# A two-layer hybrid block and a mixture of experts: units of the first gate moved into gated linear attention, three sparse items left without a weight unit

## The reference

```python
def hybrid_mixer(h, ...):
    (hq, hf, hi, hog, gq, gk, gv, glr, gog,
     nq_, nkc, nvc, nks, nvs, nkw, nvw, ngate, mgate) = split_cols(h @ w_in)
    ...
    y_hg = head_rmsnorm(o_hg, hg_norm_g, h.dtype) * jax.nn.silu(hog)
    log_a = jax.nn.log_sigmoid((glr @ gla_w2 + gla_b).astype(jnp.float32)) / GLA_TAU
    o_gla = chunked_gated_linear_attention(heads(gq, GLA_HEADS) * GLA_DK ** -0.5, heads(gk, GLA_HEADS),
                                           heads(gv, GLA_HEADS), heads(log_a, GLA_HEADS))
    y_gla = head_rmsnorm(o_gla, gla_norm_g, h.dtype) * jax.nn.silu(gog)
    ...
    y_nsa = nsa_attention(q, kc, vc, ks, vs, kw, vw, gates)
    g = jax.nn.sigmoid(mgate).reshape(B, T, N_BRANCH, D_MODEL)
    m = (g[:, :, 0] * (y_hg @ w_br_hg) + g[:, :, 1] * (y_gla @ w_br_gla)
         + g[:, :, 2] * (y_nsa @ w_br_nsa))
    return m @ w_out
```

## Time and profile before

| quantity | value |
|---|---|
| median of 3 runs | 2077.39 us (2074.11 to 2078.36) |
| the profiled execution's own time | 2070.91 us |
| its span, first to last instruction | 2069.1 us |
| TensorE busy, share of the span | 1986.2 us, 96% |
| VectorE busy | 1446.2 us, 70% |
| ScalarE busy | 1035.8 us, 50% |
| mean granted TensorE clock | 0.986 |
| second linear attention to the start of the rotation, layer 0 | about 136 to 196 us |
| sparse items, layer 0 | about 245 to 328 us |

### The profile page before, as it was taken

The page is one execution under the profiler, slowest core; times in us unless marked ns, Lnnn a source line. Parts: engine busy times, 40 slices in busy tenths (PEclk is TensorE's granted clock), DMA queues, the critical chain, the costliest instruction groups (busy, mean ns, idle before and its releaser), DMA issues.

```text
span 2069.1 us, 40471 instructions
## 1 busy us (share of the span) xinstructions
PE 1986.2 (96%) x17190; PEld 1942.8 (94%) x17190; DVE 1446.2 (70%) x2389; ACT 1035.8 (50%) x1480; POOL 8.7 (0%) x17
## 2 busy tenths in 40 slices
PE   7899999999989999999999899999899999999998
PEld 7899999999989899999999889999889999999998
DVE  5867777787578777768756757777759775665554
ACT  5754554544375555545444454444366664444443
POOL 0000000000000000000000000000000000000000
PEclk9999999999999999999999999999999999999999
DMA  6433533697544343348865236788725423365552
GB/s 208 132 114 103 194 113 132 216 321 260 182 143 133 124 158 118 124 173 285 305 203 191 92 109 227 292 310 295 287 90 174 154 94 111 122 202 187 192 193 93
DMA packets 101844, 370.18 MB, mean 179 GB/s; under 512 B 11552, under 2 KB 11936, under 8 KB 101536
## 3 DMA queue, kind: packets, MB, share of 16 engines
q1 hardware_dynamic: 100368, 363.38, 51.7%
q10 hardware_dynamic: 1296, 4.21, 0.6%
HBM read 366.50 MB, written 1.05 MB: 178 GB/s over the span
## 4 chain that ended last, share of the span: by engine, by line
PE 57%; DVE 22%; DMA 9%; ACT 7%; issue 5%; SPq 0%; ACTq 0%; DVEq 0%
PE ps L378 15%; PE ps L380 15%; PE ps L379 15%; DVE low L315 7%; DMA ada_rows<-in_ada 5%; DMA raw<-in_stream 4%; ACT high L312 3%; DVE ada_rows L2107 3%; PE ps L609 1%; DVE sq L3058 1%; PE ps L658 1%; PE ps L2039 1%; PE ps L1599 1%; PE ps L3143 1%; PE ps L912 1%
## 5 line engine op out<-in xcount | busy, mean ns | idle before, releaser
L315 DVE TENSOR_TENSOR low<-raw,high 128x1024 fp32r<-128x1024 f32 x590 | 717.6, 1221 | 368.5 <-ACT high L312 367.5
L378 PE MATMUL ps<-hh,high 128*128 128x256 f32 x2832 | 803.6, 284 | 23.2 <-DVE low L315 16.0
L312 ACT CAST high<-raw 128x1024 fp32r<-128x1024 f32 x590 | 612.7, 1047 | 423.9 <-PE ps L380 324.1
L379 PE MATMUL ps<-hh,low 128*128 128x256 f32 x2832 | 788.4, 278 | 0.0
L380 PE MATMUL ps<-hl,high 128*128 128x256 f32 x2832 | 788.2, 278 | 0.0
L378 PEld LDWEIGHTS ps<-hh,high 128*128 128x128 f32 x2832 | 535.5, 189 | 32.7 <-issue 17.6
L379 PEld LDWEIGHTS ps<-hh,low 128*128 128x128 f32 x2832 | 535.6, 189 | 1.2 <-issue 0.5
L380 PEld LDWEIGHTS ps<-hl,high 128*128 128x128 f32 x2832 | 535.7, 189 | 0.0
L378 PE MATMUL ps<-ffn_high,high 128*128 128x256 f32 x672 | 192.1, 286 | 4.2 <-DVE ffn_low L2126 4.2
L379 PE MATMUL ps<-ffn_high,low 128*128 128x256 f32 x672 | 189.3, 282 | 0.0
L380 PE MATMUL ps<-ffn_low,high 128*128 128x256 f32 x672 | 189.2, 281 | 0.0
(11 more groups left out here) (468 smaller groups left out, 2816.6 us busy)
## 6 DMA issues: line engine op xcount, KB each, us to landing
raw<-in_stream SPq DMA_DIRECT2D x590, 512.0 KB, 4.2
ada_rows<-in_ada SPq DMA_DIRECT2D x96, 512.0 KB, 5.4
c_act<-in_c SPq DMA_DIRECT2D x3, 512.0 KB, 4.3
bias<-in_bias ACTq DMA_DIRECT2D x1, 1536.0 KB, 8.7
xT<-in_xT SPq DMA_DIRECT2D x4, 256.0 KB, 5.6
out<-xT SPq DMA_DIRECT2D x4, 256.0 KB, 2.1
par<-in_par ACTq DMA_DIRECT2D x1, 842.0 KB, 11.2
hybrid_const<-in_const ACTq DMA_DIRECT2D x1, 800.0 KB, 5.9
```

The lines of the kernel that those rows point to most:

```text
L312: return act.copy(self.high[:, slot, :], self.raw[:, slot, :])
L315: return dve.tensor_tensor(self.low[:, slot, :], self.raw[:, slot, :], self.high[:, slot, :].bitcast(F32), ALU.subtract)
L378: pe.matmul(out, sh, mh, start=start, stop=False, **more)
L379: pe.matmul(out, sl, mh, start=False, stop=False, **more)
```

## The change

In the second linear attention the plan is filled differently: step 0 has three units instead of two, steps 1 to 6 have one each, step 7 none, and step 8 the second half of the last pair; the pair that stood between the sums of squares and the spreading is gone from there. All constant products of this call go (6, 9 and 3 a layer). The first two units of `Mix`, the two halves of the first gate, move into the end of this stage: TensorE does one before the values and one after them, and ScalarE and VectorE treat both at the very end of their programs for this stage. The gate's result goes to a bank of `banks` instead of `mix_banks`. `rope` keeps three units (the next three), `compress` has eight instead of seven, `compressed_probabilities` three, and the sparse items 16 instead of 19: items 4, 7 and 10 have none. The ring gets 11 units of mix before the compression's weights instead of 8. The first linear attention, which calls the same function, stays as it was.

```diff
+            gates_ahead = mix.take(2) if mix is not None else ()
...
                     for p in tail[1:]:
                         proj.vector(dve, p)
+                    for p in gates_ahead:
+                        mix.vector(dve, p)
...
                     for p in tail[1:]:
                         proj.scalar(act, p)
+                    for p in gates_ahead:
+                        mix.scalar(act, p)
...
                         for p, only in plan[step]:
                             proj.tensor(pe, mine[p], only)
+                    for p in gates_ahead[:1]:
+                        mix.tensor(pe, p)
...
                     tell(ins, pv_done)
-                    keep_busy(pe, 6, 3)
+                    for p in gates_ahead[1:]:
+                        mix.tensor(pe, p)
+                    if mix is None:
+                        keep_busy(pe, 6, 3)
...
-                        self.gate[n] = Product(w, i * BLOCKS, 2, KD, mix_banks)
+                        self.gate[n] = Product(w, i * BLOCKS, 2, KD, mix_banks if n else banks)
...
-                return self.mine[0:2] if i < 0 else self.mine[i + 2:i + 3]
+                return [p for p, at in zip(self.mine, (-1, -1, 0, 1, 2, 3, 5, 6, 8, 9, 11, 12, 13, 14, 15, 16)) if at == i]
...
-            mine, last = taken[:5], taken[5:]
+            mine, last = taken[:6], taken[6:]
...
+            mix = Mix()
+            mix.claim(11)
             linear_attention(gq, gk, gv, gg, GLA_H * GLA_DK // P, GLA_DK, gog, P1("gla_norm", layer), 1, proj,
-                             [[(0, None)], [(1, 0)], [(1, 1)], [(2, 0)], [(2, 1)], [], [], [], [(3, None)]], 1,
-                             {1: 6, LEVELS: 9})
+                             [[(0, None), (1, 0)], [(1, 1)], [(2, 0)], [(2, 1)], [(3, 0)], [(3, 1)], [(4, 0)], [], [(4, 1)]], 0,
+                             {}, mix)
...
-            mix = Mix()
-            mix.claim(8)
             windows = ring.claim(4)
-            mix.claim(len(MIX_ORDER) - 8)
+            mix.claim(len(MIX_ORDER) - 11)
             rope(mix, 3)
-            compress(windows, mix, 5 + 2)
+            compress(windows, mix, 6 + 2)
             compressed_probabilities(mix, 3)
-            sparse_attention(mix, 19)
+            sparse_attention(mix, 16)
```

10 lines of the change are left out of this document (6 added, 4 removed).

## The result

| | kernel before | changed kernel |
|---|---|---|
| median of 4 runs each, taken together | 2075.87 us | 2097.66 us (2092.77 to 2105.49) |
| ratio | | 1.0104, 95% interval 1.0085 to 1.0123 |
| the profiled execution's own time | 2070.91 us | 2092.77 us |
| its span | 2069.1 us | 2091.0 us |
| mean granted TensorE clock | 0.986 | 0.979 |

The change makes the kernel 1.0% slower. The span grew by 21.9 us where the sum had 14.1.

The account below looks back on a forecast made before the run. TensorE, busy 1986.2 of 2069.1 us, was taken as the bound. Layer 0 +2.6, layer 1 +4.5 and clock +7.0 made +14.1 on 2077.4, so 2091.5 us, range 2079 to 2098.

Parts of the forecast that it names:

- the sum: Whole kernel: layer 0 +2.6, layer 1 +4.5 and clock +7.0, together +14.1 us.
- the walk: Second linear attention, step by step: TensorE waits 0.6, 1.0 and 1.5 us for VectorE; sums of squares start at 187.1.
- Second linear attention: Constants go, two units come in, VectorE decides the rest; stage ends at 191.5 instead of 192.74: -1.2 us a layer.
- Spreading takes 1.7: End of the second linear attention: spreading was to take 1.7 us, ending the stage at 191.5.
- Rotation, layer 0: Late rotation makes TensorE wait 3.0 us for the fourth unit's weight split; windows' products start at 223.4: +4.6 us.
- Rotation, layer 1: TensorE waits 4.9 us at the rotation's start until the tanh has read bank 3: +6.5 us.
- Sparse items: Items 4, 7 and 10 without a unit wait 3.3, 1.8 and 3.0 us, later waits shrink: -2.0 us a layer.
- The clock: Six new waits of about 3 us or more bring five falls to half clock at 1.4 each: +7.0 us.
- Rival 1: The granted clock holds after the new waits: +7.1, 2084.5 us; chance 0.17.
- rival 3: TensorE's own work decides everywhere, only the linear attention counts: -13.6, 2063.8 us; chance 0.12.
- Rival 2: Waits at the rotation do not show, clock falls only in the sparse items: about +3, 2080.6 us; chance 0.10.
- Rival 4: Table switches cost the Trainium skill's 2.66 us, delaying split and bank in both layers: +2.8, 2094.3 us; chance 0.06.

Follow-up runs that it names:

- Experiment 7: Kernel before with only the new step plan, plus three or two constant products ahead of the wait before the spreading: ratios 0.9958 and 0.9943.
- Experiment 2: Changed kernel with the first gate of layer 1 in PSUM bank 1 instead of 3: 2092.42 us, ratio 1.0067.
- Experiment 6: Changed kernel with constant products in the sparse items' three waits: too many 2102.67 us (1.0117), sized to fit 2089.36 us (1.0047).
- experiment 3: Changed kernel with the two gate units' ScalarE and VectorE work moved ahead, behind the deviation's reciprocal: 2085.12 us, ratio 1.0038.
- the plan alone: Kernel before with only the second linear attention's new step plan, its 6 and 9 constants gone, no units moved in: 2069.32 us, ratio 0.9956.
- the early gate: Changed kernel with the gate units' ScalarE and VectorE work behind the deviation's reciprocal instead of at the stage's end: 2085.12 us, ratio 1.0038.
- experiment 8: Kernel before with the new step plan, two constants before the spreading and four before each hybrid layer's dense network: 2065.10 us, ratio 0.9929.

## Why the prediction came out as it did

The mechanisms were found and most sizes held, but the time is inside the range by 0.3 us of 19, and the sum was 7.8 us short in the profiled execution. That the range held was in part luck.

**Second linear attention: right.** Waits of 0.15, 0.97 and 1.14 us for the 0.6, 1.0 and 1.5 of the walk, the sums at 186.36 for 187.1, the wait before the spreading 0.81 for 1.0. The spreading starts at 189.01 where the sum had 189.8. The step that failed is the next: "Spreading takes 1.7". It took 3.43, at a granted clock of 0.50 in both layers. The constants that the change removes had a use that I did not price: they stood before thin work. So the stage ends at 192.20, 0.5 us earlier than before and not 1.2. Experiment 7 shows the price at this place (1.7 us).

**Rotation, layer 0: the mechanism right, the term mis-sized.** ScalarE's and VectorE's queues went as worked out, within a microsecond (rotation at 199.39 for 198.6, first branch at 208.28 for 207.5). TensorE resumed at 209.03, for which the sum had 209.3. But it had been stopped one unit earlier. The sum made it wait for the split of the fourth unit's weights; in fact the third unit behind the rotation's products is the second branch's, which writes the mix bank that the first branch's combination still has to be read from, and VectorE does that combination at 208.28. In the kernel before the two gate units are ahead of it in the same place, so it comes fifth and never waits. One unit more behind the wait is 2.8 us: the wait was 4.76, not 3.0, and the windows' products started at 227.04, not 223.4 (2.5 of the 3.6 are this, the rest the half clock from 209.0). I looked at weights only, and not at the banks, although the prediction had found exactly such a bank wait in layer 1.

**Rotation, layer 1: right on the bank, short behind it.** 4.93 us for 4.9, at the place and for the reason named. Behind it came the second branch's wait again, 1.45 us where the sum had the unit "about ready", and 6.8 us of half clock for the 3.4 that it counted. Experiment 2 shows that the bank's wait was not a term by itself: taken away, 3.2 of its 4.9 us came back as the wait for `hk`.

**Sparse items: right.** Waits of 2.89, 1.09 and 3.18 us for 3.3, 1.8 and 3.0. The turn of item 14 comes 70.07 us after that of item 0 in layer 0 (260.30 to 330.37) for 66.9 and two falls at 1.4, 69.7. Experiment 6, with the falls away, gives 70.5 us from first to last transposition for all sixteen where the kernel before takes 72.2 and 72.0: the -2.0 of the sum is -1.6.

**The clock: price right, places wrong.** The price of 1.4 us a fall held (1.4 and 1.8 in experiment 6). Counted were five falls behind six waits. There were five behind these six (209.0, 284.1, 314.8, 744.9, 864.4; the wait of 2.80 in layer 1 had none, like the 2.90 of the earlier trace rows), but one of them was twice as long, and three more came behind waits of 0.8 us and in the compressed probabilities (188.5, 738.1 and 246.5). Those three and the longer one are 5.6 us at 1.4. Part of the places is chance: the wait of 2.90 in the earlier trace rows, from which the prediction argued, has no fall behind it in the kernel before, but nine of the thirteen traces have one behind the same wait of 2.8 or 2.9 us. In the changed kernel:

```profile
1193.88 0.52 PE L1621 MATMUL ps<-const,probs 128*128 128x128 f32 x3 [2.90 <-DVE probs L1664]
```

```profile
1195.50:1198.90 3.40, 3.40 (x11) 2.85 (x10) 3.23 (x13) 0.88 (x4) 0.00 (x0) 0.51 0.48 154
```

**Sum.** 14.1 predicted in the profiled execution; 2.5 for the bank in layer 0, 1.45 for it in layer 1, and 5.6 for the clock's further falls make 23.7, against 22.1 in the two layers and 21.9 in the span (2.0 us of the long fall lie within the bank's wait and cost nothing). That the span to median step was taken as 6.5 us, and came out as 4.9, took 1.6 back; so the median missed by 6.2.

**Rivals.** Rival 1 (the clock holds) and rival 3 (TensorE alone decides) are out by the windows and by every wait above. Rival 2 asked whether the waits at the rotation would show; they do, but experiment 3 shows that they hang on where the two gate units' ScalarE and VectorE calls stand; which of the two engines' calls matters more is not shown, since they were moved together. Rival 4, the table switch at 2.66 us: the rounding before it ends at 195.38, the load starts at 195.39 and the tanh at 196.69, 1.30 us later, so the row's price holds. The 2.66 us of the Trainium skill (ScalarE: Activation LUTs, What ACT_TABLE_LOAD costs) does not show here.

## What to carry to other kernels

A unit that is pulled forward takes its result bank and its ScalarE and VectorE calls with it: walk the banks' readers as closely as the weights', since the unit that stops is the next one to use the bank, which may be the one after the one moved. Work may be taken out of a serial chain only where other work of TensorE (here the value products) still covers the step; measured, the same three units cost 4 us a layer less from odd items. And where the clock falls behind thin stretches, constants sized to the wait, not over it, gained some 0.5% without moving any work. Before a difference of a microsecond or two between two traces is put down to an edit, count the products in a stretch without waits in both.

## What was not expected of the hardware

- A wait of 0.81 us was followed by 3.4 us of half clock (188.5, 738.1; 185.6 and 721.5 with the plan alone), while waits of 2.80 and 2.90 us were not. Around the wait of 0.81 TensorE does thin work: products of 128x1 before, of 128x128 after. Of the sixteen such waits in the eight traces that have them fifteen were followed by a fall (layer 1 of the early gate was not); with two or three constants in it, none of eight was.
- Where the clock falls differs between executions of the same code: behind the wait of 2.90 us in nine of thirteen traces, and at 233.3 with two constants at the spreading but not in experiment 8, whose code is the same up to there. So one trace does not show that a fall which was prevented has moved, and the falls of one layer can't be priced one by one from it.
- At full granted clock and without waits a unit's products start 113 or 118 ns apart (x708 and x681 in the same 80 us of two executions), which over a dense network comes to 5 us or more, as much as three falls.
- A constant is two rows of TensorE, 0.43 us together; with twice the intended length of filling the gain was gone (2102.67 against 2089.36 us).
- Useless products in a wait of 3 us made the kernel faster, by 1.4 to 1.8 us for each fall of the clock that they kept away.
